# Row maxima subtracted as four extra contraction rows, a down projection with the activations stationary, and re-ordered vector, scalar and Pool work in the attention

## The chip, the cores and the metric

The kernel runs on one core of a Trainium2 chip. The metric is the device time of one execution in microseconds; three runs of the kernel before took 1431.07, 1431.39 and 1433.14 us (median 1431.39). Five engines work side by side, each with its own instruction queue, and wait for one another by semaphores: TensorE (PE, matrix products), VectorE (DVE), ScalarE (ACT), GpSimd (POOL) and SyncE (SP, here only the issuer of DMAs).

## The reference

Two layers of a bidirectional encoder trunk on x of 512 tokens by 1024 channels, everything in float32. The part that the change touches is the softmax of two attention groups and the last projection:

```python
p = h @ W_in                       # hyena channels | GQA q, k, v | MLA q-rank, kv-rank, rope key
# GQA: 8 query heads, 2 kv heads, d 64.   MLA: 4 heads, nope 64 + shared rope 32, v 64
s  = einsum(q, k) * scale          # per head, 512 queries x 512 keys
pr = softmax(s, axis=-1)           # subtracts the row maximum
o  = einsum(pr, v)
y  = concat(rms(hyena), rms(gqa), rms(mla)) @ w_out
x += rms_norm(y, mix_post_norm)
f  = (gelu(dwconv3(h @ W_g)) * dwconv3(h @ W_u)) @ w_down      # 2816 -> 1024
x += rms_norm(f, ffn_post_norm)    # the last layer's x is the output
```

## The kernel before, in words

Activations lie transposed in SBUF, channels on partitions: `xT` is [128, 8, 512], chunk c holding channels 128c to 128c+127 of all 512 tokens. A product in float32 accuracy is made of three products of a faster type (fp32r): operand and weight are each split into a rounded high part and a low remainder, and `triple` or `tiles` (L1105 to L1107, L1138 to L1140) issue high x high, high x low and low x high. Weights come in items of at most 8 tiles of 128x128: SP loads an item into `raw` (two slots), ScalarE rounds it into `wh` (`hi`, L611), Pool takes the remainder `wl` (`lo`, L527). Some items (`third`) use a third pair of buffers, `xh` and `xl`; `freed` says after which item a buffer may be overwritten. Nothing is scheduled by a planner: each engine's program is written out by hand, in Python loops, and its order is the order of the queue.

**Attention.** The 12 heads (8 GQA, then 4 MLA) run one after the other, each in two passes. In the first, `peaks(h, ...)` (L1304) makes the scores of 128 queries at a time, with queries on the partitions, in banks 0 and 1; VectorE takes each row's negated maximum into `nm[:, h % 2, qc]` (`maxima`, L1816). In the second, `scores(h, sc)` makes the same scores with 128 keys on the partitions and all 512 queries along the row, so that `exp` gives the transposed probabilities that the product with V wants. The maximum belongs to a column there, so it cannot be a bias of the exponential. It is added in the product: Pool multiplies the identity with the maxima, `shift(h)` (L564), into `diag`, [128, 512], whose column q holds only the maximum of query q, and TensorE adds `ones_r` times `diag` to each score tile (L1328). A GQA tile is therefore three products of 512 columns (`ka` x `Q2`, `kb` x `Q2`, `ones_r` x `diag`), where `Q2[h % 3]` stacks the high and the low part of q on the two halves of the partitions and `ka`, `kb` hold the key's high and low part twice. An MLA tile is one full float32 product (L1325) and the `diag` product. While head h's score tiles are made, the `peaks` of head h+1 are made between them. `values` (L1445) are the products with V of a pair of heads, `denominators` (L1456) the sums over keys, from `row_sums` of VectorE (L1826); `bank7` makes the MLA projections in nine pieces between the heads; `group(g)` (L1401), `group_square`, `group_sum`, `group_norm`, `group_hi` and `group_lo` are the RMSNorm of the three groups ahead of `w_out`.

**The last down projection.** As in the first layer, output chunk m (of 8) is accumulated over the 22 chunks of the hidden activations `fh`, `fl` with weights stationary and 512 tokens moving: 8 x 22 x 3 matmuls. Chunk 7 is done in two halves of 256 tokens (`last_item`), so that the norm of the first half can start while the second is made. Then follow the sum of squares over partitions (`stat_post`, L1090 and L1093), the root on ScalarE (`post`), gain times root and the residual (`last_stream`, with Pool's `add` taking every second chunk), the turn back to tokens on partitions with 32 transposes of 128x128 (L1576), the copies to `xout` (L1027) and eight DMAs of 256 KB.

## Time and profile before

| | |
|---|---|
| median of 3 runs | 1431.39 us |
| the profiled execution, its own time | 1426.5 us |
| span, first to last instruction | 1424.7 us |
| mean granted clock of TensorE | 0.994 of full speed |
| PE busy | 1368.3 us, 96% of the span |
| DVE, ACT, POOL busy | 915.4, 587.7, 554.1 us |

The matmuls are pipelined: the profile gives each its full latency, so that the durations of neighbours overlap, and what one costs in a row of them is the distance from its start to the next start. A full float32 product appears as two matmul records. The attention of the first layer lies at about 166 to 292 us, that of the second at 864 to 993 us; the last down projection ends at 1411 us.

### The profile page before, as it was taken

The page shows a single profiled execution, that of the slowest core. Times are in us where ns is not written, and L with a number is a line of the kernel's source. Part 1 is how long each engine was busy: PE and PEld are TensorE (multiplying, and loading weights), DVE is VectorE, ACT ScalarE, POOL GpSimd, SP SyncE. Part 2 cuts the span into 40 slices and gives each one's busy share as a digit, 9 for nine tenths or more (in the row PEclk, how much of TensorE's full clock was granted, in tenths as well). Part 3 has the DMA queues.
Part 4 walks back from the last instruction along what each step waited for, and adds up shares of the span by engine and source line. Part 5 has one row for each costly group of instructions (what it writes and reads, how often), then busy time and mean ns, then how long its engine had stood idle before and what let it go on. Part 6 is the DMA issues. An engine that isn't in the chain of part 4 may idle for free. (4 is left out here: it accounts for less than half of the span.)

```text
span 1424.7 us, 15494 instructions
## 1 busy us (share of the span) xinstructions
PE 1368.3 (96%) x5988; PEld 1027.0 (72%) x5988; DVE 915.4 (64%) x992; ACT 587.7 (41%) x864; POOL 554.1 (39%) x287
## 2 busy tenths in 40 slices
PE   7999989999999999999989998998999999999998
PEld 5587654378888888788866785444888888887886
DVE  6776976547777787611286788665478877874213
ACT  5322455545543434422352225454464344343323
POOL 3221333046444444444552224320554444444444
PEclk9999999999999999999999999999999999999999
DMA  7313201022233333233341222110223333333332
GB/s 250 97 30 81 67 10 52 1 61 73 85 94 95 97 89 103 82 93 95 101 143 49 60 49 57 30 30 15 75 75 89 89 99 94 89 99 87 92 97 84
DMA packets 205538, 112.53 MB, mean 79 GB/s; under 512 B 15303, under 2 KB 202425, under 8 KB 204570
## 3 DMA queue, kind: packets, MB, share of 16 engines
q1 hardware_dynamic: 205466, 111.54, 27.0%
q8 instruction: 48, 0.79, 0.2%
q14 instruction: 24, 0.20, 0.0%
HBM read 105.63 MB, written 2.10 MB: 76 GB/s over the span
## 5 line engine op out<-in xcount | busy, mean ns | idle before, releaser
L527 POOL TENSOR_TENSOR wl<-raw,wh 128x1024 fp32r<-128x1024 f32 x172 | 421.5, 2451 | 628.2 <-ACT wh L611 628.2
L611 ACT ACTIVATE wh<-raw 128x1024 fp32r<-128x1024 f32 x172 | 182.1, 1059 | 519.8 <-PE ps L1140 493.8
L1138 PE MATMUL ps<-gh,wh 128*128 128x512 f32 (+1 forms) x848 | 340.7, 402 | 0.0
L1140 PE MATMUL ps<-gh,wl 128*128 128x512 f32 (+1 forms) x848 | 334.7, 395 | 0.0
L1139 PE MATMUL ps<-gl,wh 128*128 128x512 f32 (+1 forms) x848 | 334.6, 395 | 0.0
L1138 PEld LDWEIGHTS ps<-gh,wh 128*128 128x128 f32 (+1 forms) x848 | 158.3, 187 | 43.3 <-issue 3.9
L1139 PEld LDWEIGHTS ps<-gl,wh 128*128 128x128 f32 (+1 forms) x848 | 158.3, 187 | 40.5 <-issue 2.4
L1140 PEld LDWEIGHTS ps<-gh,wl 128*128 128x128 f32 (+1 forms) x848 | 158.2, 187 | 39.1
L1599 DVE TENSOR_TENSOR acc<-acc,sq 128x512 f32<-128x512 f32 x24 | 60.2, 2510 | 190.1 <-ACT sq L655 190.1
L2030 DVE SCALAR_TENSOR_TENSOR cv<-pad,pm,cv 128x512 f32<-128x512 f32 x88 | 127.4, 1447 | 70.0 <-ACT cv L989 70.0
L1138 PE MATMUL ps<-fh,wh 128*128 128x512 f32 x308 | 121.7, 395 | 0.6 <-POOL wl L527 0.6
L1139 PE MATMUL ps<-fl,wh 128*128 128x512 f32 x308 | 121.5, 395 | 0.0
L1140 PE MATMUL ps<-fh,wl 128*128 128x512 f32 x308 | 121.5, 395 | 0.0
L2017 DVE TENSOR_TENSOR fl<-fprod,fh 128x512 fp32r<-128x512 f32 x44 | 98.9, 2247 | 13.2 <-ACT fh L1006 13.2
L1816 DVE TENSOR_REDUCE nm<-ps 128x1 f32<-128x512 f32 x96 | 64.0, 687 | 42.5 <-PE ps L1304 42.0
L564 POOL TENSOR_TENSOR diag<-ident,nm 128x512 fp32r<-128x512 f32 x24 | 28.9, 1204 | 128.7 <-DVE nm L1816 66.5
L2033 DVE SCALAR_TENSOR_TENSOR cv<-pad,pm,cv 128x512 f32<-128x512 f32 x88 | 70.5, 802 | 3.1
L989 ACT ACTIVATE cv<-pad,pm 128x512 f32<-128x512 f32 x88 | 70.5, 803 | 0.0
L1138 PEld LDWEIGHTS ps<-fh,wh 128*128 128x128 f32 x308 | 58.0, 188 | 15.0 <-issue 1.5
L1140 PEld LDWEIGHTS ps<-fh,wl 128*128 128x128 f32 x308 | 58.0, 188 | 13.6
L1139 PEld LDWEIGHTS ps<-fl,wh 128*128 128x128 f32 x308 | 58.0, 188 | 13.5
L2025 DVE TENSOR_TENSOR pad<-ps,rbc 128x512 f32<-128x512 f32 x88 | 56.4, 683 | 8.1 <-ACT rbc L622 8.1
(288 smaller groups left out, 2242.0 us busy)
## 6 DMA issues: line engine op xcount, KB each, us to landing
raw<-w_up SPq DMA_DIRECT2D x86, 512.0 KB, 3.8
raw<-w_down SPq DMA_DIRECT2D x32, 512.0 KB, 3.8
raw<-w_in SPq DMA_DIRECT2D x30, 512.0 KB, 4.1
raw<-w_out SPq DMA_DIRECT2D x16, 512.0 KB, 3.8
raw<-w_down SPq DMA_DIRECT2D x16, 384.0 KB, 3.4
xio<-x SPq DMA_DIRECT2D x4, 512.0 KB, 4.7
win<-c_win SPq DMA_DIRECT2D x2, 1024.0 KB, 5.5
TF<-c_tf SPq DMA_DIRECT2D x2, 1024.0 KB, 8.7
```

Source lines behind the costliest of these rows:

```text
L527: nc.gpsimd.tensor_tensor(l, raw[:, slot, :], h.bitcast(F32), ALU.subtract).then_inc(S["lo_ready"], 1)
L611: A(xh[:] if third(lay, n) else wh[:, slot, :], raw[:, slot, :], ACT.Copy).then_inc(S["hi_ready"], 1)
L989: A(cv[:, k, :], pad[:, k, 1:T + 1], ACT.Identity, scale=pm[:, bass.ds(col + j + (PM["ffn_w1"] + k * FC), 1)], bias=pm[:, bass.ds(col + j ...
L1138: mm(ps[0:cols, bank, :], w_hi, x_hi, start=start and k == 0, stop=False)
L1139: mm(ps[0:cols, bank, :], w_hi, x_lo, start=False, stop=False)
L1140: ins = mm(ps[0:cols, bank, :], w_lo, x_hi, start=False, stop=stop and k == tile_n - 1)
L1599: tt(acc[:], acc[:], sq[:, m % 2, :], ALU.add).then_inc(S["ysq_used"], 1)
L1816: nc.vector.reduce_max(nm[:, h % 2, qc:qc + 1], ps[:, N_BANK(h, qc), :], AX.X, negate=True).then_inc(S["nmax"], 1)
L2017: tt(fl[:, j:j + 1, :], fprod[:].rearrange("p (o t) -> p o t", o=1), fh[:, j:j + 1, :].bitcast(F32), ALU.subtract).then_inc(S["f_lo"], 1)
L2025: tt(pad[:, k, 1:T + 1], ps[:, UP_BANK(j, k), :], rbc[:], ALU.mult).then_inc(S["f_evac"], 1)
L2030: V.do(stt(out=c, in0=pad[:, k, 0:T], scalar=pm[:, bass.ds(col + j + (PM["ffn_w0"] + k * FC), 1)], in1=c, op0=ALU.mult, op1=ALU.add))
L2033: stt(out=c, in0=pad[:, k, 2:T + 2], scalar=pm[:, bass.ds(col + j + (PM["ffn_w2"] + k * FC), 1)], in1=c, op0=ALU.mult, op1=ALU.add).then_i ...
```

## The change

**Maxima as rows.** After the fourth `maxima` of a head, TensorE turns `nm[:, h % 2, :]`, [128, 4], with the identity into [4, 128] (`turn_maxima`), right behind `scores(h - 1, 3)`. VectorE multiplies this by a block identity into four rows of 512 (`max_row`): row c holds the maxima of queries 128c to 128c+127 in its own 128 columns and zeros elsewhere. These rows lie under the queries (partitions 64 to 67 of the new buffer `q3` for GQA, 96 to 99 of `mqf` for MLA), and four rows of ones lie under the keys, in `kb` and `mkf`. The `diag` product and Pool's `shift` are gone. For GQA the second product is now the key's low part (64 rows) with the whole q, copied by Pool into `q3` (`q_again`), plus the four rows. `klo` writes `kb` twice instead of four times, and the ones.

```diff
+                def turn_maxima(h):
+                    pe.wait_ge(S["nmax"], lay * N_TILES + (h + 1) * TC)
+                    mm(ps[ROW(h), N_BANK(h, TC - 1), 0:P], nm[:, h % 2, :], ident[:], start=True, stop=True).then_inc(S["nm_tr"], 1)
+
                     if h < GH:
                         mm(ps[:, bank, :], ka[:, h // 4, keys], Q2[h % 3], start=True, stop=False)
-                        mm(ps[:, bank, :], kb[:, h // 4, keys], Q2[h % 3], start=False, stop=False)
+                    if sc == 0:
+                        ...
+                        pe.wait_ge(S["nm_row"], lay * HEADS + h + 1)
+                    if h < GH:
+                        ins = mm(ps[:, bank, :], kb[row, h // 4, keys], q3[row, h % 2, :], start=False, stop=True)
                     else:
-                        mm(ps[:, bank, :], mkf[0:MD, h - GH, keys], mqf[0:MD, h - GH, :], start=True, stop=False)
-                    if sc == 0:
-                        pe.wait_ge(S["shift"], lay * HEADS + h + 1)
-                    mm(ps[:, bank, :], ones_r[:], diag[:, h % 2, :], start=False, stop=True).then_inc(S["s_tile"], 1)
+                        ins = mm(ps[:, bank, :], mkf[row, h - GH, keys], mqf[row, h - GH, :], start=True, stop=True)
+                    ins.then_inc(S["s_tile"], 1)
...
+                def max_row(h):
+                    rows = ROW(h)
+                    dst = q3[rows, h % 2, :] if h < GH else mqf[rows, h - GH, :]
+                    ...
+                    dve.wait_ge(S["nm_tr"], lay * HEADS + h + 1)
+                    tt(dst.rearrange("p (c n) -> p c n", c=TC),
+                       ps[rows, N_BANK(h, TC - 1), 0:P].unsqueeze(1).to_broadcast([TC, TC, P]),
+                       ident[rows, rows].unsqueeze(2).to_broadcast([TC, TC, P]), ALU.mult).then_inc(S["nm_row"], 1)
```

**Orders.** On VectorE each `max_row(h + 1)` stands behind `maxima(h + 1)`, at heads 4, 6, 8 and 10 behind `pair_out` too, at head 7 behind a copy of `bank7`; `row_sums(1)` moves behind `maxima(4)`, `row_sums(9)` and `row_sums(10)` into head 11; the group sums move ahead of the `row_sums` of their head; `group_norm(1)` is split in two. Two of the four low parts of the MLA weights (`uql`, `ukl`) move from VectorE to Pool. On Pool the two first `w_out` items move from the beginning and the middle of the attention behind head 9. On ScalarE the group squares move ahead of `inverse` and `group_hi(1)` is split. On TensorE one quarter of the last `values` comes ahead of `denominators(4)`.

On TensorE, head 3 of the first layer and what stands just ahead of it, before (q2 is a slot of `Q2`):

```order
L1328 MATMUL ps<-diag,ones_r 128x512
L1445 MATMUL ps<-probT0,vg 64x512
L1445 MATMUL ps<-probT1,vg 64x512
L1445 MATMUL ps<-probT0,vg 64x512
L1445 MATMUL ps<-probT1,vg 64x512
L1322 MATMUL ps<-q2,ka 128x512 [waits p_ready]
L1323 MATMUL ps<-q2,kb 128x512
L1328 MATMUL ps<-diag,ones_r 128x512 [waits shift]
L1304 MATMUL ps<-ka,q2 128x512 [waits q2lo,q2hi,nmax]
L1304 MATMUL ps<-ka,q2 128x512 [waits nmax]
```

and now:

```order
L1393 MATMUL ps<-ident,nm 4x128 [waits nmax]
L1543 MATMUL ps<-probT0,vg 64x512
L1543 MATMUL ps<-probT1,vg 64x512
L1543 MATMUL ps<-probT0,vg 64x512
L1543 MATMUL ps<-probT1,vg 64x512
L1412 MATMUL ps<-q2,ka 128x512 [waits p_ready]
L1420 MATMUL ps<-q3,kb 128x512 [waits nm_row,q3]
L1388 MATMUL ps<-ka,q2 128x512 [waits q2lo,q2hi,nmax]
L1388 MATMUL ps<-ka,q2 128x512 [waits nmax]
```

The product with `diag` is gone from each tile, the turn of the maxima stands once per head ahead of the products with V, and the tile's second product carries the wait for the rows.

On VectorE, from the end of `maxima(4)` (head 3) to the reductions of the next head, before:

```order
L1816 TENSOR_REDUCE nm<-ps 128x1 [waits n_tile] x3
L1826 TENSOR_TENSOR tsum<-uc 128x1024 [waits den_mm,p_ready]
L1930 TENSOR_TENSOR yt<-kr,rope 32x512 [waits kr_in]
L1931 TENSOR_TENSOR yt<-krs,rope 32x512
L1933 TENSOR_TENSOR kr<-yt 32x512 [waits dve_self]
L1816 TENSOR_REDUCE nm<-ps 128x1 [waits n_tile,shift,dve_self]
```

and now:

```order
L1910 TENSOR_REDUCE nm<-ps 128x1 [waits n_tile] x3
L1920 TENSOR_TENSOR tsum<-probT1 128x1024 [waits p_ready]
L1894 TENSOR_TENSOR q3<-ps,ident 4x512 [waits nm_tr]
L1902 TENSOR_TENSOR ckl<-ckv,ckh 128x512 [waits mhi]
L2025 TENSOR_TENSOR yt<-kr,rope 32x512 [waits kr_in]
L2026 TENSOR_TENSOR yt<-krs,rope 32x512
L2028 TENSOR_TENSOR kr<-yt 32x512 [waits dve_self]
L1920 TENSOR_TENSOR tsum<-uc 128x1024 [waits den_mm,p_ready,dve_self]
L1910 TENSOR_REDUCE nm<-ps 128x1 [waits n_tile,nm_tr]
```

`row_sums(1)` (tsum from probT1), which `denominators(0)` waits for, now stands between the maxima of head 4 and their row, and `ckl` has come here too.

**The last down projection.** In the last layer an item is now the 128 rows of one hidden chunk kk with all 1024 output channels, 22 items in place of 24. `last_down` holds the activations still (128 hidden by 128 tokens) and moves 512 output channels: all 8 banks accumulate at once, bank 2tt + dh for token block tt and half dh, and the last two chunks (`TAIL`) are done bank by bank. The output has tokens on the partitions; `xT` is turned beforehand, in 8 groups of four transposes between the up projection's items (`turn_stream`), and ScalarE copies each to `xres`. Item LAST (kk 21) uses `xh`, `xl`.

```diff
+            def last_down(lay):
+                def part(kk, tt, dh):
+                    h, l = weights(lay, I_DOWN + kk)
+                    bank, rows, cols = 2 * tt + dh, slice(tt * P, (tt + 1) * P), slice(dh * T, (dh + 1) * T)
+                    mm(ps[:, bank, :], fh[:, kk, rows], h[:, cols], start=kk == 0, stop=False)
+                    mm(ps[:, bank, :], fl[:, kk, rows], h[:, cols], start=False, stop=False)
+                    return mm(ps[:, bank, :], fh[:, kk, rows], l[:, cols], start=False, stop=kk == FC - 1)
+                ...
+                for kk in range(FC - TAIL):
+                    ready(kk)
+                    for tt in (0, 2, 3, 1):
+                        ...
+                        for dh in range(2):
+                            ins = part(kk, tt, dh)
+                    ins.then_inc(S["pe_item"], 1)
+                for kk in range(FC - TAIL, FC):
+                    ready(kk)
+                for tt in range(TC):
+                    for dh in range(2):
+                        for kk in range(FC - TAIL, FC):
+                            ins = part(kk, tt, dh)
+                        ins.then_inc(S["y_done"], 1)
...
+            for tt in range(TC):                                   # ScalarE
+                s0, s1, part, log, r = (st[:, tt, i:i + 1] for i in range(5))
+                act.wait_ge(S["y_done"], 2 * tt + 1)
+                C.do(A(yt[:, 0, :], ps[:, 2 * tt, :], ACT.Square, accum_out=s0))
+                ...
+                C.do(A(yt[:, 1, :], ps[:, 2 * tt + 1, :], ACT.Square, accum_out=s1))
+                ...
+                C.do(A(log, s1, ACT.Ln, bias=part, scale=1.0 / DM))
+                C.join()
+                A(r, log, ACT.Exp, scale=-0.5).then_inc(S["r_inv"], 1)
...
+            for i in range(TC):                                    # VectorE
+                for dh in range(2):
+                    dve.wait_ge(S["y_sq"], 2 * i + dh + 1)
+                    ...
+                    tt(ytmp[dh], ps[:, 2 * i + dh, :], cv[:, dh, :], ALU.mult).then_inc(S["y_gain"], 1)
+                dve.wait_ge(S["r_inv"], i + 1)
+                for dh in range(2):
+                    dve.wait_ge(S["y_gain"], 2 * i + dh + 1)
+                    x = xres[2 * i + dh]
+                    stt(out=x, in0=ytmp[dh], scalar=st[:, i, 4:5], in1=x, op0=ALU.mult, op1=ALU.add).then_inc(S["o_done"], 1)
```

The sum over channels is now along the row, so ScalarE takes it while squaring; `stat_post`, `last_stream`, Pool's adds, the transposes of the tail and the copies to `xout` are gone. At the program's end TensorE has, before (the last triple of chunk 7, its statistics, the first of the 32 transposes):

```order
L1090 MATMUL ps<-acc,ones_r 128x256 [waits rms_post]
L1093 MATMUL ps<-sq,ones_r 128x256 [waits ysq]
L1576 MATMUL ps<-ident,xT 128x128 [waits x_own]
L1576 MATMUL ps<-ident,xT 128x128
L1576 MATMUL ps<-ident,xT 128x128 [waits x_new]
```

and now (the bank-by-bank end: wh is item kk 20, xh item kk 21):

```order
L1239 MATMUL ps<-wh,fh 128x512 [waits hi_ready,lo_ready,f_lo,f_hi]
L1240 MATMUL ps<-wh,fl 128x512
L1241 MATMUL ps<-wl,fh 128x512
L1239 MATMUL ps<-xh,fh 128x512
L1240 MATMUL ps<-xh,fl 128x512
L1241 MATMUL ps<-xl,fh 128x512
```

Nothing of TensorE's follows these six once they have been made for the eighth bank.

## Rows read from the trace of the kernel before

**Rows 1.** Waits of PE, whole run: total us, times, longest (the attention's lines).

```profile
PE ps L1401 <- DVE acc L1909: 5.7, 6, 1.2
PE ps L1304 <- DVE nm L1816: 5.4, 6, 1.5
PE ps L1328 <- POOL diag L564: 4.4, 4, 1.9
PE ps L1304 <- POOL q L555: 2.9, 3, 1.3
PE ps L1138 <- DVE yl L1924: 2.8, 2, 1.4
PE ps L1456 <- ACT cv L622: 1.7, 2, 0.8
PE ps L1322 <- DVE kb L1801: 1.5, 2, 1.0
```

**Rows 2.** Both attentions by window: length, busy (count) by engine, PEclk, DMA.

```profile
166.00:292.00 126.00, 113.50 (x425) 57.84 (x425) 82.79 (x109) 66.53 (x113) 31.95 (x23) 0.99 0.08 24
864.00:993.00 129.00, 115.87 (x428) 59.17 (x427) 83.11 (x109) 67.26 (x113) 32.41 (x23) 0.97 0.09 24
...
184.00:186.00 2.00, 2.00 (x7) 1.57 (x6) 1.51 (x3) 1.12 (x2) 0.00 (x0) 0.54 0.00 0
```

**Rows 3.** Timeline, PE, head 2 to 3: start us, us, instruction.

```profile
198.38 0.39 PE L1304 MATMUL ps<-ka,q 128*128 128x512 f32 x1
...
199.08 0.40 PE L1328 MATMUL ps<-diag,ones_r 128*128 128x512 f32 x1
```

**Rows 4.** Timeline, DVE: the maximum of the product that starts at 198.38.

```profile
198.81 0.69 DVE L1816 TENSOR_REDUCE nm<-ps 128x1 f32<-128x512 f32 x1 [0.24 <-PE ps L1304]
```

**Rows 5.** Timeline, PE: two MLA score tiles of the last head, start to start.

```profile
272.40 1.02 PE L1325 MATMUL ps<-mqf,mkf 96*128 96x512 f32 x2
...
273.49 1.02 PE L1325 MATMUL ps<-mqf,mkf 96*128 96x512 f32 x2
```

**Rows 6.** Timeline, PE: four 128x128 transposes and the next product.

```profile
164.07 0.60 PE L1375 MATMUL ps<-ident,cv 128*128 128x128 f32 x4
164.50 0.59 PE L1279 MATMUL ps<-sq,ones_r 128*128 128x512 f32 x1
```

**Rows 7.** Timeline, PE: denominators of a pair, and the next score product.

```profile
222.81 1.94 PE L1456 MATMUL ps<-tsum,ones_r 128*64 128x512 f32 x8
224.68 0.50 PE L1322 MATMUL ps<-q,ka 128*128 128x512 f32 x1
```

**Rows 8.** DVE: 32 partitions from PSUM (timeline); row sums (group: busy, mean ns).

```profile
176.28 0.68 DVE L1691 SCALAR_TENSOR_TENSOR kr<-ps,rbc 32x512 f32<-32x512 f32 x1
...
L1826 DVE TENSOR_TENSOR tsum<-probT 128x1024 f32<-128x1024 f32 x9 | 12.9, 1435 | 4.3 <-PE ps L1456 4.3
```

**Rows 9.** Timeline, PE and ACT, the end of the program.

```profile
1408.10 0.59 PE L1090 MATMUL ps<-acc,ones_r 128*128 128x256 f32 x2
...
1408.78 0.47 PE L1105 MATMUL ps<-fh,xh 128*128 128x256 f32 x1
...
1411.12 0.59 PE L1090 MATMUL ps<-acc,ones_r 128*128 128x256 f32 x2
...
1421.81 0.38 ACT L1027 ACTIVATE xout<-ps 128x256 f32<-128x256 f32 x1 [0.29 <-PE ps L1576]
```

**Rows 10.** Timeline, ACT and DVE: 512-column operations as in the new tail.

```profile
159.93 0.63 ACT L763 ACTIVATE sq<-cq 128x512 f32<-128x512 f32 x1 [3.86 <-DVE cq L1694]
...
175.50 0.75 DVE L1775 SCALAR_TENSOR_TENSOR cq<-cq,pm,rr 128x512 f32<-128x512 f32 x1
```

**Rows 11.** The last down projection's items: rounding, remainder, landing of a load.

```profile
1312.43 1.06 ACT L611 ACTIVATE wh<-raw 128x1024 fp32r<-128x1024 f32 x1 [4.51 <-PE ps L1140]
...
1313.57 2.40 POOL L527 TENSOR_TENSOR wl<-raw,wh 128x1024 fp32r<-128x1024 f32 x1 [3.16 <-ACT wh L611]
...
raw<-w_down SPq DMA_DIRECT2D x32, 512.0 KB, 3.8
```

More of the change, by code:

```diff
@@ L264, in build @@
         ysave = probT0
+        xres = [rope[:, i, :] for i in range(5)] + [w3[:, 0:T], w3[:, T:2 * T], h2[:, 0:T]]
+        ytmp = [sq[:, 0, :], sq[:, 1, :]]
         groot = [rbc[:], cv[:, 1, :], rbc[:]]
@@ L492, in _ @@
                     item(lay, I_UP + 2 * j + 1, w_up[bass.ds(lay, 1), :, :, bass.ds(DFF + j * P, P)])
+                if lay == DEPTH - 1:
+                    for kk in range(FC):
+                        item(lay, I_DOWN + kk, a["w_down"][lay:lay + 1, kk * P:(kk + 1) * P, :].rearrange("o p (c n) -> o p c n", n=P))
+                    sp.wait_ge(S["f_prod"], DEPTH * FC)
+                    sp.dma_start(cv[:].rearrange("p t n -> p (t n)"), a["ffn_post_norm"][lay, :].partition_broadcast(P)
+                                 ).then_inc(S["g_in"], 16)
+                    continue
                 for m in range(0, DC - 1, 2):
@@ L529, in add @@
             def add(lay, b):
-                last = (lay, b) == (DEPTH - 1, 1)
                 for half in range(2):
                     for c in range(DC):
-                        if (c % 2 == 0 if last else c == half == 0):
+                        if c == half == 0:
                             continue
@@ L594, in _ @@
                 add(lay, 0)
-                for n in range(I_UP + 2, ITEMS + 1 if lay < DEPTH - 1 else ITEMS - 1, 2):
+                for n in range(I_UP + 2, ITEMS + 1 if lay < DEPTH - 1 else LAST, 2):
                     for slot in range(2):
@@ L861, in group_root, with group_hi @@
                     act.wait_ge(S["gstd"], lay * 3 + g + 1)
-                def group_hi(g):
+                def group_hi(g, cs=None):
                     src, _, n, c0 = GROUPS[g]
-                    for c in range(n):
+                    for c in cs or range(n):
                         act.wait_ge(S["y_norm"], lay * DC + c0 + c + 1)
@@ L1009, in _ @@
                 tables("natural_log_exp_and_others")
+                if lay == DEPTH - 1:
+                    for n in range(I_DOWN + 3, LAST + 1):
+                        hi(lay, n, n % 2)
+                    continue
                 for m in range(DC):
@@ L1909, in group_sum, with group_norm @@
                         tt(acc[:], acc[:], sq[:, k % 2, :], ALU.add).then_inc(S["gsq_used"], 1)
-                def group_norm(g):
+                def group_norm(g, cs=None):
                     src, _, n, c0 = GROUPS[g]
                     dve.wait_ge(S["gstd"], lay * 3 + g + 1)
-                    for c in range(n):
+                    for c in cs or range(n):
                         stt(out=src[:, c, :], in0=src[:, c, :], scalar=par("g_out", c0 + c), in1=groot[g], op0=ALU.mult,
@@ L1963, in _ @@
                         maxima(h + 1)
+                    if h == 3:
+                        row_sums(1)
+                    if h == 2 or h % 2 and h + 1 < HEADS and h != 7:
+                        max_row(h + 1)
                     if h in B7_FIRST and B7[B7_FIRST[h]][0] in ("pe", "v"):
@@ L1967, in _ @@
                         pair_out((h - 4) // 2)
-                    if h:
+                        if h + 1 < HEADS:
+                            max_row(h + 1)
+                    if h == 7:
+                        max_row(h + 1)
+                    if h == 3:
+                        mla_lo(1)
+                        rotate_kr()
+                    if h == 5:
+                        group_sum(0)
+                        group_sum(1)
+                    if h == 9:
+                        group_sum(2)
+                        group_sum(3)
+                    if h == 10:
+                        group_sum(5)
+                    if h == 11:
+                        group_norm(1, [0, 1])
+                    if h not in (0, 2, 11):
                         row_sums(h - 1)
```

230 lines of the change are left out of this document (126 added, 104 removed).

## The prediction, made before the changed kernel was run

> **What bounds the kernel now.** I read the busy shares first: TensorE (PE) is busy 96% of the span at a mean clock of 0.994, the others at most 64%. PE's program is therefore the path, and a term counts only as PE time taken away or added, PE waiting, PE's clock, or the start and the tail of the program. Next I read PE's waits [rows 1]: the seven rows that belong to the attention sum to 24.4 us over both layers (5.7 + 5.4 + 4.4 + 2.9 + 2.8 + 1.7 + 1.5), none above 1.9. Then the windows over both attentions [rows 2]: PE clock 0.99 and 0.97, VectorE (DVE) busy 83 of 126 us, Pool 32. And then the timeline of the end [rows 9]: the last product of the down projection is over at 1411.12, the last copy starts at 1421.81, the span ends at 1424.7. All sums are made against the profiled execution's own 1426.5 us; the median of the runs lies 4.9 us above it, and I carry that over.
>
> **The change part by part.**
>
> *The product with `diag`.* From 198.38 to 199.08 three matmuls start, 0.233 us each [rows 3]. Twelve heads, four tiles, two layers make 96 of the removed ones: 96 x 0.233 = 22.4 us less. Four more contraction rows in the remaining product, and 68 in place of 128 rows in the second GQA product, cost nothing: time goes by the moving columns, since the 96-row MLA product with its `diag` product takes 1.09 us a tile [rows 5], that is 0.86 for 512 columns of full float32.
>
> *The turn of the maxima.* 24 full float32 products of 128 columns. None is in the trace; a quarter of 0.86 is 0.215, and with its whole latency exposed it would be about 0.5. I take 0.22, the nearer row: +5.2 us (bounds 5 to 12). It cannot be below nothing, as it is an added instruction.
>
> *The new waits.* The turn waits for the fourth maximum. A product that starts at 198.38 has its maximum at 198.81 + 0.69 = 199.50 [rows 4], while PE, after that product and the two of a GQA tile, is ready 3 x 0.233 later, at 199.08: 0.42 us, about 0.47 with the semaphore, at the eight heads where the tile before the turn is GQA. At MLA heads PE has 0.23 + 0.86 = 1.09 us of its own and waits for nothing. That makes 3.8 us a layer. What queues behind the turn on PE is the products with V or the denominators; who waits for it is only `max_row`. `max_row` itself reads PSUM and writes 4 partitions of 512; the nearest row, 32 partitions of 512 from PSUM, takes 0.68 [rows 8], and bounds of 0.4 and 1.0 change little: the denominators of a pair take 1.87 us on PE [rows 7], and the turn and the row (0.22 + 0.68 and two semaphores, about 1.1) go by beside them. Only at head 1, where nothing but one product lies between, is some 0.5 us open, and it takes the place of the 1.9 us wait for Pool [rows 1].
>
> *The other stops, per layer.* What I count as left: 0.4 at the first `peaks`; 1.4 at head 0, because the norm of `cq` and the copy of `kr` still stand ahead of `maxima(1)`; 0.5 for the row of head 1; 1.0 for `cql`, now behind that row; 1.3 at head 3, where the rotary work of `bank7` stands ahead of `maxima(4)`; 1.0 at `denominators(0)`, since `row_sums(1)`, 1.4 us by the mean [rows 8], now comes behind `maxima(4)`, less the turn; 1.0 at `group(2)`; 0.5 for the rest. With the 3.8 above it is 10.9 a layer, 21.7 in all against 24.4: -2.7 us. Gone are the group sums of groups 0 and 1, the wait for Pool's low part of q, the wait for `yl` and that for the root ahead of the denominators. The bounds are wide: -17 if only the turn's wait stays, +10 if the queue of VectorE falls behind.
>
> *VectorE and Pool.* VectorE takes on 12 x 0.68 = 8.2 us a layer and loses two low parts and two of four `kb` operations; at most 91 us [rows 2] in an attention of some 114. Pool loses 12 products and gains 8 copies of half the partitions; at 32 us of 126 [rows 2] nothing waits for it but the first heads. Both are free as long as their slack lies where it is needed.
>
> *The clock.* The granted clock fell to 1.2 GHz after the 1.9 us wait in the first layer (0.54 granted in 184 to 186 [rows 2]), and both windows together lost (1 - 0.99) x 126 + (1 - 0.97) x 129 = 5.1 us. With waits of at most 1.4 us I give back two thirds: -3.4 us (bounds 0 and -5.1, and a loss of as much again if the new row of short waits brings it down more often).
>
> *The turn of x.* 32 transposes between the up projection's items. Four of them start at 164.07 and the next product at 164.50 [rows 6]: 0.108 each, +3.4 us. The copies stand on ScalarE, less than half busy there. The Trainium skill ("TensorE: Matmul & The Clock Gate", Part 4: PE-mode transpose) gives about 275 ns for one in a kernel's context; by its figure the term would be 8.8 us. The row here shows the start-to-start distance, which is what counts in a queue, and I go by it.
>
> *The down projection.* The same number of full products, 22 x 8 x 3. The two halves of chunk 7 go: 132 products of 256 columns at 0.120 against 66 at 0.233, and the statistics between them, 1408.10 to 1408.78 [rows 9]: -1.1 us together. An item is 24 products, 5.6 us, and needs 1.06 + 2.40 us of ScalarE and Pool [rows 11], so PE does not wait in the row. The end does: chunks 20 and 21 must both be ready when 19 is done. The slot of 21 is free when the remainder of 19 is, 3.6 us after PE left 17; the load lands 3.8 us later [rows 11], and Pool can start on 21 only behind 20, at about 9.3, ending at 11.8 when PE is there at 11.2: +0.6 us. At the start of the projection, banks of the last up items are touched last (token block 1 at 4.2 us into the first item): nothing.
>
> *The tail.* Before, 1424.7 - 1411.12 = 13.6 us. Now, after the last product: 0.2 until ScalarE starts, a square 0.63 [rows 10], the logarithm and the exponential of one column (not in the trace; between 0.17 and 0.42 each, I take 0.25) with their joins 0.7, two operations of 0.75 on VectorE [rows 10], and from the last release to the end as before, 1424.7 - 1421.81 - 0.38 = 2.5 us [rows 9]. This is 5.5; VectorE's own row, with a product from PSUM behind the last square, adds 0.3: 5.8 us, -7.8. Bounds 4.8 and 8.5, the second if VectorE (2 x 0.68 + 2 x 0.75 = 2.9 us for a token block) is late against PE's 12 x 0.233 = 2.8.
>
> **Sum.** -22.4 + 5.2 - 2.7 - 3.4 + 3.4 - 1.1 + 0.6 - 7.8 = -28.2: own time 1398.3 us, median 1403.2.
>
> **The rivals.**
>
> *A, VectorE sets the pace.* Its chain through a head (four maxima, row, row sums, and what stands between) is then the longest, and the `diag` time comes back as PE waiting. For it: the largest attention waits are for VectorE [rows 1], and it takes on 8 us. Against: 83 of 126 us busy [rows 2]. The three attention terms would cancel, leaving -3.4 - 4.9: 1423.
>
> *B, all stops go but the turn's.* The order was moved at each row of [rows 1], and PE's own time around the pair products (1.87 us against four times 0.43 [rows 5, 7]) makes PE later, and so VectorE earlier, than I count. Another 14.2 us: 1389.
>
> *C, slower: the round trip is on the path at every head.* PE, VectorE, PE, VectorE, PE follow one another once per head. If VectorE has other work ahead of `max_row`, as `pair_out` is at four heads and `row_sums` at one, the row comes after the pair products: 0.7 for what stands ahead, and 0.9 for turn and row uncovered, 24 x 1.6 = 38 us. 1403 + 38 = 1441. From 28.2 / 24 = 1.2 us a head the change is lost. Against it: 1.87 us of cover [rows 7], and the largest thing ahead of a row is row sums at one head.
>
> *D, transposes are not pipelined between other products.* By the length of the first row of [rows 6], 0.60 for four of which three distances are 0.32, each would cost 0.28, +5.4 us: 1409. The Trainium skill's 275 ns ("TensorE: Matmul & The Clock Gate", Part 4: PE-mode transpose) would come to the same.
>
> *E, the change does not do what it says*: if the last down projection with its eight open banks stalls at each chunk by the 1.06 + 2.40 us of its preparation, because buffers come free later than I read, the 7.8 us are used up from 0.4 us a chunk. 1411.
>
> **How the numbers follow.** The forecast 0.58 (its own range 1394 to 1411), A 0.13, B 0.13, C 0.06, D 0.06, E 0.04. Less than 0.2% (2.9 us, about what this measurement tells from nothing) is left only between A and C. Faster 0.92, same 0.03, slower 0.05. For 8 times in 10 the range reaches to B, and towards A without holding it: 1390 to 1420.
>
> **What would show it.** Right: no product of `ones_r` with a [128, 512] tile; about 0.45 us of PE waiting for VectorE's maxima ahead of each of eight turns a layer; no wait for the rows above 0.6 us but at the first heads; attentions 11 to 12 us shorter each; transposes 0.11 us apart; about 0.6 us of waiting once, ahead of the last two chunks; 5.8 us from the last product to the end. Wrong: PE waits for `max_row` at most heads (C), VectorE busy over 85% of the attention and PE waiting for maxima within a head (A), PE waits for Pool inside the last projection (E), or a mean clock below 0.97 in either attention.

## The result and the profile after

| | before | after |
|---|---|---|
| median of the runs, us | 1431.23 (1431.06 to 1433.14, 4 runs) | 1396.65 (1393.99 to 1399.51, 4 runs) |
| ratio, 95% interval | | 0.9756 [0.9732, 0.978] |
| profiled execution, its own time, us | 1426.5 | 1398.35 |
| its span, us; mean granted clock | 1424.7; 0.994 | 1396.6; 0.993 |

Faster by 34.6 us; the forecast was 1403.2 by the median and 1398.3 by the profiled execution's own time. The second came out to 0.1 us, which is luck: as shown below, the waits fell by 5.4 us more than forecast, while the turn of the maxima, the clock between the layers and the layout of the operands together came out some 8 us dearer.

TensorE's waits in the changed kernel (whole run; us in total, times, longest), to be laid beside [rows 1]:

```profile
PE ps L1144 <- DVE gl L1681: 7.3, 14, 1.6
...
PE ps L1388 <- DVE nm L1910: 5.2, 6, 1.5
PE ps L1393 <- DVE nm L1910: 5.1, 16, 0.3
...
PE ps L1554 <- DVE tsum L1920: 2.6, 2, 1.3
...
PE ps L1388 <- POOL q L576: 1.4, 2, 0.8
...
PE ps L1496 <- DVE acc L2004: 1.1, 2, 0.6
PE ps L1420 <- DVE q L1894: 0.9, 2, 0.4
PE ps L1239 <- POOL xl L549: 0.8, 1, 0.8
```

The attention's rows (L1388, L1393, L1554, L1496, L1420) now sum to 16.3 us against 24.4. New is L1393, the turn: sixteen waits, eight a layer as forecast, of 0.3. The waits for `diag`, `kb`, `yl` and for the roots are gone, and four of the six for group sums. `cql`, for which the forecast had 1.0 a layer, does not appear.

The windows over both attentions, then the place between the layers (window, its length, busy time and count per engine, PE's clock, DMA), beside [rows 2]:

```profile
166.00:278.00 112.00, 103.74 (x399) 48.98 (x400) 85.38 (x118) 66.08 (x112) 25.28 (x22) 1.00 0.10 28
855.00:968.00 113.00, 104.82 (x398) 48.93 (x398) 85.38 (x118) 66.09 (x112) 24.65 (x22) 0.98 0.10 28
700.00:726.00 26.00, 22.90 (x110) 17.95 (x111) 23.55 (x39) 13.78 (x26) 16.25 (x15) 0.80 0.53 182
```

The first attention runs at 1.00. But between the layers, where the kernel before had 1.00 in the same window, the clock is 0.80: half of the time spent at 1.2 GHz is 5.1 us there, in a stage that the change does not touch.

```profile
700.00:726.00 26.00, 22.62 (x161) 20.03 (x160) 16.64 (x32) 12.71 (x24) 17.63 (x17) 1.00 0.53 184
```

TensorE's timeline at the turn of head 1 (start, length, line, tiles, idle time before and its releaser), beside [rows 3]:

```profile
179.15 0.40 PE L1420 MATMUL ps<-q,kb 68*128 68x512 f32 x1
179.86 0.38 PE L1393 MATMUL ps<-ident,nm 128*4 128x128 f32 x2 [0.31 <-DVE nm L1910]
180.18 0.50 PE L1412 MATMUL ps<-q,ka 128*128 128x512 f32 x1
181.12 0.47 PE L1420 MATMUL ps<-q,kb 68*128 68x512 f32 x1 [0.44 <-DVE q L1894]
```

From 179.15 to 179.86 are 0.71, less the product's 0.23 are 0.48: the forecast's 0.47 (the view shows 0.31 of it as idle, since it lets the product end later). The turn itself takes 0.32 before the next product starts (179.86 to 180.18), where the forecast had 0.22. No third product of [rows 3] follows a score's second, and the one of 68 rows still costs one 0.23 (the median over the 32 that a product of `peaks` follows). The turn of x, beside [rows 6], and the wait ahead of chunks 20 and 21 (the four transposes last 0.60 together and stand 0.109 apart, so that one alone lasts 0.60 - 3 x 0.109 = 0.27):

```profile
1072.77 0.60 PE L1231 MATMUL ps<-ident,xT 128*128 128x128 f32 x4
1073.12 0.48 PE L1177 MATMUL ps<-gh,wh 128*128 128x512 f32 x1
```

```profile
1379.91 0.47 PE L1239 MATMUL ps<-wh,fh 128*128 128x512 f32 x1 [0.77 <-POOL xl L549]
```

And the end of the program, beside [rows 9]:

```profile
1390.86 0.40 PE L1241 MATMUL ps<-xl,fh 128*128 128x512 f32 x1
...
1391.29 0.60 ACT L1070 ACTIVATE yt<-ps 128x512 f32<-128x512 f32 x1 [0.29 <-PE ps L1241]
...
1391.79 0.19 ACT L1070 ACTIVATION_READ_ACCUMULATOR yt<-ps 128x1 f32 x1
1392.06 0.69 DVE L2163 TENSOR_TENSOR sq<-ps,cv 128x512 f32<-128x512 f32 x1 [0.15 <-ACTq L1072]
1392.10 0.30 ACT L1073 ACTIVATE st<-st 128x1 f32<-128x1 f32 x1
1392.42 0.20 ACT L1075 ACTIVATE st<-st 128x1 f32<-128x1 f32 x1
1392.66 0.75 DVE L2168 SCALAR_TENSOR_TENSOR w<-sq,st,w 128x512 f32<-128x512 f32 x1
1393.33 0.74 DVE L2168 SCALAR_TENSOR_TENSOR h<-sq,st,h 128x512 f32<-128x512 f32 x1
```

The last product is over at 1391.09 (its start and 0.23), the span at 1396.55: 5.5 us against 13.6.

### The profile page after: what moved, and what is told of

Same layout as the page of the kernel before. It is cut to its first block, busy times and chain, and to the rows that moved or that the text cites. A ratio compares the mean times of both kernels' runs of the same rounds, so it can differ in the third digit from the quotient of the medians.

```text
span 1396.6 us, 15257 instructions
## 1 busy us (share of the span) xinstructions
PE 1352.3 (97%) x5866; PEld 1006.3 (72%) x5866; DVE 899.8 (64%) x995; ACT 583.7 (42%) x865; POOL 531.9 (38%) x275
## 4 chain that ended last, share of the span: by engine, by line
PE 77%; DVE 14%; ACT 2%; issue 2%; POOL 2%; DMA 1%; SPq 1%; POOLq 0%; DVEq 0%; ACTq 0%
PE ps L1177 16%; PE ps L1178 16%; PE ps L1179 16%; PE ps L1239 3%; PE ps L1240 3%; PE ps L1241 3%; DVE nm L1910 2%; PE ps L1543 2%; PE ps L1338 2%; PE ps L1312 2%; PE ps L1422 2%; PE ps L1554 1%; DVE p L1817 1%; PE ps L1388 1%; DVE gl L1681 1%
## 5 line engine op out<-in xcount | busy, mean ns | idle before, releaser
L549 POOL TENSOR_TENSOR wl<-raw,wh 128x1024 fp32r<-128x1024 f32 x170 | 417.3, 2455 | 684.4 <-ACT wh L640 672.8
L1690 DVE TENSOR_TENSOR acc<-acc,sq 128x512 f32<-128x512 f32 x18 | 45.2, 2511 | 112.7 <-ACT sq L684 112.7
L2120 DVE TENSOR_TENSOR fl<-fprod,fh 128x512 fp32r<-128x512 f32 x44 | 95.0, 2159 | 17.7 <-ACT fh L1042 17.7
L2163 DVE TENSOR_TENSOR sq<-ps,cv 128x512 f32<-128x512 f32 x8 | 5.5, 688 | 104.0 <-ACTq L1067 102.9
L1239 PE MATMUL ps<-wh,fh 128*128 128x512 f32 x168 | 66.5, 396 | 1.0 <-POOL xl L549 0.8
L1241 PE MATMUL ps<-wl,fh 128*128 128x512 f32 x168 | 66.3, 395 | 0.0
L1240 PE MATMUL ps<-wh,fl 128*128 128x512 f32 x168 | 66.3, 395 | 0.0
L1177 PE MATMUL ps<-fh,wh 128*128 128x512 f32 x154 | 61.0, 396 | 0.3 <-POOL wl L549 0.3
L1179 PE MATMUL ps<-fh,wl 128*128 128x512 f32 x154 | 60.9, 396 | 0.0
L1178 PE MATMUL ps<-fl,wh 128*128 128x512 f32 x154 | 60.9, 396 | 0.0
```

Of the source, the lines that this page charges most:

```text
L549: nc.gpsimd.tensor_tensor(l, raw[:, slot, :], h.bitcast(F32), ALU.subtract).then_inc(S["lo_ready"], 1)
L1177: mm(ps[0:cols, bank, :], w_hi, x_hi, start=start and k == 0, stop=False)
L1178: mm(ps[0:cols, bank, :], w_hi, x_lo, start=False, stop=False)
L1179: ins = mm(ps[0:cols, bank, :], w_lo, x_hi, start=False, stop=stop and k == tile_n - 1)
L1239: mm(ps[:, bank, :], fh[:, kk, rows], h[:, cols], start=kk == 0, stop=False)
L1240: mm(ps[:, bank, :], fl[:, kk, rows], h[:, cols], start=False, stop=False)
```

## The experiments

All times are medians. Each kernel ran beside the kernel before on the same chip, which gave 1428.22 us (17 runs, from 1423.3 to 1432.93) beside `again`, `attn_only`, `down_only` and `no_diag`, 1426.31 (15) beside `st8`, `turn_cover`, `old_orders` and `dve_load`, 1427.76 (11) beside `before_pad`, `st12` and `st24`, and 1427.49 (9) beside `head0`. A stage table, worked out from starts of instructions and the clock records of each profiled execution, serves all of them. Each entry is the stage's length, and behind it the time lost in it at 1.2 GHz (half of the time spent there), both in us. An attention is counted from its first `peaks` to `group(2)`, the output and up projection from there to the first down product.

| kernel | attention 0 | attention 1 | output and up 0 | output and up 1 | down 0 | last product to end |
|---|---|---|---|---|---|---|
| before | 124.5, 1.7 | 127.1, 3.4 | 293.9 | 294.7 | 124.4 | 13.7 |
| after | 110.7, 0 | 112.3, 1.7 | 294.9 | 298.3 | 124.8 | 5.7 |
| again | 112.7, 3.4 | 111.8, 1.7 | 294.9 | 298.3 | 124.8 | 5.7 |
| attn_only | 111.3, 1.7 | 110.3, 0 | 293.9 | 293.9 | 124.4 | 14.0 |
| down_only | 127.2, 3.4 | 125.3, 1.7 | 294.9 | 298.3 | 124.8 | 5.7 |
| no_diag | 120.2, 1.7 | 119.9, 3.4 | 293.9 | 293.9 | 124.5 | 15.0 |
| old_orders | 126.5, 5.1 | 127.4, 6.8 | 295.0 | 298.3 | 124.8 | 5.7 |
| dve_load | 116.1, 3.4 | 117.2, 5.1 | 294.9 | 298.3 | 124.8 | 5.7 |
| before_pad | 127.7, 3.4 | 125.2, 1.7 | 288.0 | 288.0 | 122.3 | 14.0 |
| st12 | 111.3, 1.7 | 110.7, 0 | 290.3 | 293.9 | 124.4 | 5.7 |
| st8 | 112.3, 3.4 | 111.3, 1.7 | 288.0 | 291.8 | 122.4 | 5.7 |
| st24 | 111.3, 1.7 | 112.3, 3.4 | 288.0 | 291.9 | 122.3 | 5.7 |
| head0 | 110.8, 0 | 111.9, 1.7 | 288.0 | 291.8 | 122.4 | 5.7 |
| turn_cover | 111.3, 0 | 114.2, 3.4 | 294.9 | 298.3 | 124.8 | 5.7 |

The second figure is the most that the clock can have cost, not what it did cost. Up to the first `peaks`, `again` lost 3.4 us and took 167.0, `turn_cover` lost none and took 167.1. The first attention of the same orders took 110.7 with nothing lost (after), 111.3 with 1.7 (attn_only, st24) and 112.3 and 112.7 with 3.4 (st8, again). Where TensorE waits anyway, its slower products seem to fill the waits. Figures "without the clock" below are therefore somewhat low for the kernels that lost more.

**again**: no edit.

> The changed kernel once more, unchanged, to see what moves its time between runs. Theory (clock stretches): the runs of it spread over 1394 to 1400 us, and a run's time follows its mean granted clock, 0.01 of clock being 14 us of PE at a lower rate (a run at 0.999 about 1394, one at 0.990 about 1399.5); the number of stretches at 1.2 GHz between the start and the tail is not the same in each run. The kernel before should show a higher time (1431) than its profiled 1426.5 for the same reason, at a clock near 0.990 in its plain runs. Rival (what surrounds the span): all runs have the same clock within 0.002, and the spread comes from outside the span.

1396.84 (1394.92 to 1399.38). Each run's time lies 1.7 to 1.8 above its span, so what surrounds the span is constant and the rival falls. The clock goes with most of the spread, not with all: of the 17 runs of before the quickest, 1423.3, had 0.995, and those at 0.988 took 1431.5 and 1432.0; between, runs at 0.993 lie from 1427.1 to 1429.3. A straight line through the 17 gives 8.9 us for 0.01 of clock, where the expectation had 14. With the whole loss taken out (span times clock) the 17 average 1414.8 and the four of `again` 1386.5. The profiled execution of before, 1426.5, lies within these runs.

**attn_only** and **down_only**: the diff's two halves, each on the kernel before.

> Only the attention's part of the change (maxima as rows, the new orders); the last down projection and the end stay as before. Theory: the sum of the attention terms, -22.4 + 5.2 - 2.7 - 3.4 = -23.3 us, up to -28.5 by the stage windows of the changed kernel, so 1403 to 1408 against 1431. Rival 1 (the parts help each other: the attention's gain needs the other end of the program): -15 or less. Rival 2 (the attention's gain is the clock's alone and is given back between the layers): -18.

> Only the last down projection with eight open banks, the turn of x between the up items and the new end; the attention stays as before. Theory: +3.4 for the 32 transposes, -1.1 and +0.6 in the projection, -7.8 in the tail = -4.9 us: 1426. By the windows of the changed kernel -4.7 with 5.5 us from the last product to the end. Rival (the row on record calls it E, chunks stall): no gain, 1431, with PE waiting for ScalarE or Pool ahead of chunks. Rival (transposes cost 0.28 each): +5.4 more.

1398.45 (ratio 0.9795 [0.977, 0.982]) and 1422.91 (0.9964 [0.995, 0.9978]): -29.8 and -5.3 us. The attention brings more than the forecast's 23.3, the end what was forecast. The two sum to 35.1, together they bring 31.4; the spread of the runs (four of attn_only, with clocks of 0.989 to 0.996, and twelve of down_only) covers the difference, and the stages of the table show nothing that only the two together bring.

**no_diag**:

```
-  mm(..., kb[:, h // 4, keys], Q2[h % 3], start=False, stop=False)
+  mm(..., kb[:, h // 4, keys], Q2[h % 3], start=False, stop=True).then_inc(S["s_tile"], 1)
...
-  mm(ps[:, bank, :], ones_r[:], diag[:, h % 2, :], start=False, stop=True).then_inc(S["s_tile"], 1)
```

> The kernel before without the 96 products of diag, so the maxima are found but not subtracted; Pool still makes diag, and PE asks for it only at the last tile of a head. It prices the removed product by itself. Theory (PE's time is the bill): 96 x 0.233 = 22.4 us and most of the 4.4 us of waits for Pool's shift go, some 5 us of longer waits for maxima come: -20 to -25, 1406 to 1411. Rival (VectorE's maxima are nearly the pace): PE waits for nmax within heads take half of it back, 1418 to 1422.

The kernel leaves out the subtraction of the maxima, and serves to price it. 1416.47: -11.8 us, half of the 22.4 that the products took, and a little better than the rival. TensorE's waits in this kernel:

```profile
PE ps L1304 <- POOL q L555: 8.1, 10, 2.1
PE ps L1304 <- DVE nm L1815: 8.1, 8, 1.8
...
PE ps L1400 <- DVE acc L1908: 6.2, 6, 1.1
...
PE ps L1416 <- DVE cql L1807: 3.3, 2, 1.6
```

Against [rows 1] Pool's low part of q went from 2.9 to 8.1, the maxima from 5.4 to 8.1, and `cql` is new. All waits in the attentions sum to 36.5 us, against 25.2 in the kernel before (the seven of [rows 1] and one of 0.8): 11.3 of the 22.4 us come back as waiting, and 11.1 are left, which is what the runs show.

**old_orders**: the new rows and the new end, with VectorE's and ScalarE's orders of before; what was moved on Pool and TensorE stays moved.

```
                     if h and h + 1 < HEADS:
                         maxima(h + 1)
+                        max_row(h + 1)
...                      (group sums, norms, row_sums and rotate_kr where they were before)
```

> The changed kernel with the orders of VectorE and ScalarE in the attention as they were before, and each row of maxima right behind the four maxima. It parts the new rows from the new orders. Taking the product away alone (no_diag) gave 12 us and not 22, since waits for VectorE and Pool grew. Theory (the orders are worth what no_diag missed): about 1405, the group sums' waits (5.7 us) back, and waits for the rows or the denominators at even heads. Rival 1 (the rows alone bring it, the orders little): 1398. Rival 2 (C of the forecast: with the row at the wrong place the round trip is on the path): over 1415.

1427.36, ratio 1.0001 [0.9981, 1.0021] to the kernel before: 30.5 us more than `again`, and nothing left of the change. Since the new end is in it and brings 5.3 by itself, its attention is even slower than that of before (126.5 + 127.4 against 124.5 + 127.1 in the table). With the clock's loss taken out, the table gives 121.4 and 120.6 for its attentions, against 109.9 and 110.3 in the mean of after, again and attn_only: 21.8 us are waits, and the waits of the attention's lines, 37.8 us in all against 14.6 in `again`, bear that out. The clock goes with the rest: its mean over the runs is 0.9876 against 0.9938, at most 17.7 us lost against 8.7. TensorE's waits in the first attention:

```profile
PE ps L1385 <- DVE nm L1907: 7.7, 5, 3.7
PE ps L1493 <- DVE acc L2001: 4.1, 3, 1.8
PE ps L1390 <- DVE nm L1907: 2.2, 7, 0.3
...
PE ps L1417 <- DVE q L1891: 0.4, 1, 0.4
```

The time is in the range given to rival 2 (over 1415; C itself said 1441), its mechanism is not the one at work: TensorE waits 0.4 us for a row (L1417), but 3.7 at once for a maximum of head 4, behind the rotary work, `row_sums` and `ckl` in VectorE's queue, and 1.8 for a group sum.

**dve_load**: 

```
+  V.do(tt(tsum[:, h % 2, 0, :], pT[:, 0, :], pT[:, 2, :], ALU.add))
+  V.join()
   tt(tsum[:, h % 2, :, :], pT[:, 0:2, :], pT[:, 2:4, :], ALU.add).then_inc(S["summed"], 1)
```

> The changed kernel with half of each row sum computed twice, 24 more operations of about 0.7 us on VectorE, 16.8 us in all; VectorE was busy 85 of 112 us in an attention. Theory (VectorE has slack in the middle of a head, and what waits is the latency of single steps): +2 to +5 us, at denominators and at heads with bank 7 work: 1399 to 1402. Rival (A of the forecast: VectorE sets the pace): nearly all of it shows, +14 to +17: 1411 to 1414.

1407.99: +11.2 us, between the two. Of it 2.8 and 1.8 are in the attentions without the clock (112.7 and 112.1 against the same 109.9 and 110.3), as waits for the row sums:

```profile
PE ps L1554 <- DVE tsum L1922: 7.0, 4, 2.0
```

(2.1 in `again`.) The clock may have taken 3.6 more (0.9912 in the mean against 0.9938); some 3 us stay open, within the spread of four runs (1402.46 to 1408.97). VectorE has slack, but not 8 us a layer of it at this place: the added operation stands straight ahead of the row sums, and other places were not tried.

**turn_cover**: 

```
-  if after:
+  if after and h not in (5, 7, 9):
       turn_maxima(h + 1)
...
   for part in range(2):
+      if part and 1 <= p < PAIRS - 2:
+          turn_maxima(2 * p + 4)
```

> The changed kernel with three of the eleven turns behind the first two products of the denominators (heads 5, 7, 9), so that TensorE has 0.9 us of its own work while the fourth maximum comes. Theory (the forecast's wait of 0.42 us at a turn is the latency of the maximum, and the cover behind the turn is long enough): the wait of 0.31 to 0.33 us at these six turns goes and no wait for a row comes: -2.0 us, 1395. Rival (the row is then late: turn and row take some 1.2 us by now, and 0.9 + 0.23 us of products lie between): a wait for q or mqf at the next scores, 0 us or up to +1.

1396.14, no difference from 1396.84. Its waits:

```profile
PE ps L1388 <- DVE nm L1912: 6.2, 8, 1.5
...
PE ps L1393 <- DVE nm L1912: 3.8, 12, 0.3
...
PE ps L1556 <- DVE mv L2046: 1.3, 2, 0.6
```

The turn's fell from 4.8 to 3.8, those for maxima rose from 5.2 to 6.2 and one of 1.3 is new: the row is later, and VectorE's queue hands that on. Without the clock its attentions take 222.1 us, against 220.2 in the mean of after, again and attn_only. Its four runs had a higher clock, 0.998 in the mean, so the equal medians may hide a loss of some 2 us; whether the clock was chance or the edit's doing is not shown.

**st8**, **before_pad**, **st12**, **st24**: the layout alone.

```
-  st = sb("st", [P, TC, 5])
+  st = sb("st", [P, TC, 8])          (st8; 12 and 24 in st12 and st24)
```
```
   nm = sb("nm", [P, 2, TC])
+  unused = sb("unused", [P, 32])     (before_pad)
```

> The changed kernel with the statistics tile `st` of 8 columns in place of 5 (128 bytes a partition, not 80), nothing else. In the runs so far each kernel with the new end (the changed one, its repeat, the one with the end alone) starts its projection products 0.2328 us apart, those without it 0.2319: output and up projection of layer 0 take 294.9 against 293.9 us, the down projection 124.8 against 124.4. `st` lies ahead of the operands that move through TensorE (gh, gl, fh, fl, yh, yl). Theory (where the operands lie): with 128 bytes the distance is 0.2319 again, 293.9 and 124.4 in layer 0, 297.3 in layer 1, in all 2.5 to 3 us less: 1394 by the median. Rival (it is the new code on another engine, or the eight banks): 294.9 stays, 1397.

1379.71, ratio 0.9667 [0.9645, 0.9689]: -17.1 us against `again` (16 by the two ratios) and not -3. The theory named the right tile and the wrong size, so three more kernels were made to find the rule.

> The kernel before with an unused tile of 128 bytes a partition ahead of gh, nothing else. With `st` at 128 bytes (st8) the changed kernel's projection products start 0.2267 us apart and not 0.2328, and it runs 17 us shorter; it is to be seen whether that has to do with the change. Counting tiles in the order in which they are declared, rounded up to 32 bytes, wh lies at a multiple of 256 bytes, and gh at 128 beyond one before, 224 beyond one in the changed kernel, 0 beyond one in st8; products of gh with xh, whose remainders are equal in all, start 0.227 apart in all of them. Theory (equal remainders of 256 bytes for the two operands): before falls by 3312 products x 0.0052 = 17 us less some in waits, to 1411, and all products with wh and wl to 0.227. Rival (it is the tile st or the new end): 1428 stays.

> The changed kernel with `st` of 192 bytes a partition, so that gh lies 64 beyond a multiple of 256 and wh at one. Theory (equal remainders): products with wh start 0.232 to 0.233 apart as at 128 and 224, time 1394 to 1397. Rival (the remainder counts by itself, not against the other operand; 64 may be as good as 0): 0.227 or less, 1380.

> The changed kernel with `st` of 384 bytes a partition: gh now lies at a multiple of 1024 bytes, as wh does, while in st8 it lay 256 beyond a multiple of 512. Theory (256 bytes is the size that counts): as st8, 0.2267 between products and 1380. Rival (more of the address counts): shorter distances still, down to 0.2133 for 512 columns at 2.4 GHz, which would be 3400 x 0.013 = 45 us less; or longer ones.

1410.68 (0.9878 [0.9858, 0.9897]), 1388.38 (0.9714) and 1377.13 (0.9645 [0.9624, 0.9666]). An unused tile makes the kernel before 17 us faster, so this has nothing to do with the change. A window of 100 us in the up projection of layer 0, with the count of products, of before, after, st12, before_pad and st24 in turn:

```profile
400.00:500.00 100.00, 100.00 (x432) 1.00 0.33 95
```
```profile
400.00:500.00 100.00, 100.00 (x431) 1.00 0.32 92
```
```profile
400.00:500.00 100.00, 100.00 (x438) 1.00 0.32 95
```
```profile
400.00:500.00 100.00, 100.00 (x442) 1.00 0.33 95
```
```profile
400.00:500.00 100.00, 100.00 (x443) 1.00 0.33 97
```

443 products where 432 were, with the clock at 1.00 and TensorE busy throughout in all. Two rows of the timeline of st24, a triple of products apart, take 0.68 us for three, where the changed kernel's take 0.70:

```profile
500.29 0.39 PE L1177 MATMUL ps<-gh,wh 128*128 128x512 f32 x1
...
500.97 0.39 PE L1177 MATMUL ps<-gh,wh 128*128 128x512 f32 x1
```
```profile
500.21 0.40 PE L1177 MATMUL ps<-gh,wh 128*128 128x512 f32 x1
...
500.91 0.40 PE L1177 MATMUL ps<-gh,wh 128*128 128x512 f32 x1
```

Where both operands have the same remainder of 256 bytes (by the declared sizes, rounded up to 32 bytes) the distance is 0.227; at 128 apart 0.232, at 224 apart 0.2335 in the mean. st12, 64 apart, refutes the plain rule: `gl` with `wh` goes at 0.227 there, `gh` with `wl` at 0.230, `gh` with `wh` at 0.2325, and it gains half. A control stands in every kernel: the products with `xh`, whose remainder is that of `gh` whatever `st` is, have a median distance of 0.227 in before and in the changed kernel too, beside 0.232 and more for those with `wh`. st24 is st8 within the spread, and at no layout did a mean distance fall below 0.226, so its rival falls. Why the remainders matter stays open.

**head0**: on st24, VectorE's order at head 0.

```
+  copy(kb[GD:GD + TC, :, :] ...)     (the row of ones, ahead of maxima(0))
   maxima(0); klo(); max_row(0)
-  norm(5, [cq 0, cq 1]); evac(kr); maxima(1)
+  norm of cq 0; maxima(1, [0, 1]); norm of cq 1; maxima(1, [2, 3])
   max_row(1); mla_lo(0)
+  evac(kr)
```

> st24 with VectorE's order at head 0 changed: the row of ones is copied ahead of the maxima of head 0, the first two maxima of head 1 stand between the two halves of the norm of cq, and the copy of kr behind the low part of cq. In every run so far TensorE waits 1.5 us there (peaks of head 1), by VectorE's queue: norm 1.54 and kr 0.68 stand ahead of the maximum that is asked for. Theory: the wait falls from 1.5 to 0.2 us in both layers and the row of head 0 comes 0.5 us earlier; no new wait for cql: -3 to -3.5 us against st24, 1374. Rival (the next step in VectorE's queue takes the wait over: the row of head 1 or cql is late by what the first gained): 1377. Rival (the clock falls after the wait of 1.5 us, so it gives back 1.7 us a layer more): 1371.

1378.44 (0.9669 [0.9642, 0.9696]) against 1377.13: nothing. TensorE's waits name where it went:

```profile
PE ps L1412 <- ACT probT L931: 3.4, 2, 1.7
PE ps L1388 <- DVE nm L1908: 2.5, 5, 0.9
```

The 1.5 us for the maximum are gone in both layers, and 1.7 us for ScalarE's exponentials stand one product later. ScalarE, not VectorE, was the second to be late there.

## Why the prediction was right, and which terms were off

| term | forecast, us | measured, us | from |
|---|---|---|---|
| products with `diag` | -22.4 | -22.4 | 96 fewer, distances as before |
| turn of the maxima | +5.2 | +7.5 | 24 x 0.31, from a turn's start to the next product's |
| waits in the attention | -2.7 | -8.1 | 16.3 against 24.4, as the view counts them |
| clock in the attention | -3.4 | -3.4 | stage table, 5.1 to 1.7, at most |
| rest of the attention | 0 | -2.2 | what is left of the attentions' -28.6; not parted by any run |
| clock elsewhere | 0 | +3.2 | last down product of layer 0 to the second attention: 158.8, and 155.6 in again, with nothing lost |
| turn of x | +3.4 | +3.4 | 298.3 - 294.9, and 0.108 apart |
| layout of the operands | not seen | +2.4 | layer 0: 294.9 - 293.9, 124.8 - 124.4; 1.0 again in layer 1's up projection |
| last down projection | -0.5 | -0.2 | 124.5 to 124.3, wait 0.77 for 0.6 |
| tail | -7.8 | -8.1 | 13.6 to 5.5 |
| all else | 0 | -0.3 | start, stage between the layers, layer 1's projection |
| from profile to median | +4.9 | -1.7 | 1396.65 - 1398.35 |

Without its last row the measured column sums to -28.2. The attentions became 13.8 and 14.8 us shorter, where the forecast's own sign of being right was 11 to 12: it gained more there than it knew, and lost in stages that it had put at nothing.

**The waits** are the term that was mis-sized most. Nearly half of that is a way of counting. The eight turns a layer were right in number and size, 0.48 us each by distance for 0.47, but the view shows 0.32 of it as idle, so that they enter the 16.3 with 5.1 us where the forecast booked 7.5. The guesses around them came to 11.2 us for 14.2. Head 0 was right (1.5 for 1.4, and the reason given for it, the norm and `kr`, is shown by head0). Too high were `cql`, 0 for 1.0, head 3, 0.9 for 1.3, and `group(2)`, 0.55 for 1.0; too low were `denominators(0)`, 1.3 for 1.0, and the first `peaks`, 0.7 for 0.4, which still wait for the low part of q that the forecast called gone. The late work of [rows 1] was taken out of VectorE's queue more fully than the guesses allowed. The prediction named this as rival B; 3 of its 14.2 us were gone.

**The turn** cost 0.31 to 0.33 us from its start to the next product at 22 of its 24 places (at the other two the next product waits for the row sums), where 0.22 was taken, within the stated bounds of 5 to 12 us. The clock's loss and the waits being rough, the rest of -2.2 says no more than that these terms do not add up to the last us.

**The orders were priced far too low.** The forecast gave the removed product 22.4 us and all orders together 2.7. The runs show another split: product removed with the old orders, -11.8 (no_diag); rows in place of `diag` and the new end with the old orders, nothing, so that the rows alone cost more than they bring, 2.3 us by the stage table and some 6 by the medians less the end's -5.3 (old_orders); rows with the new orders, -29.8 (attn_only). What rival A described, the product's time coming back as waiting, is thus true of the old orders and false of the new ones; its reason, that VectorE is full, is not what the trace of old_orders shows, where single late steps of up to 3.7 us make the waits. The total came out because the whole diff was forecast, not its parts. Which of the moved operations brings how much is not parted.

**The clock.** In the attention its loss fell as forecast, from 5.1 to 1.7 us, but in that execution it fell elsewhere too, between the layers, which the forecast had not. `again`, the same kernel, lost nothing there and 3.4 in its first attention, where the first execution lost none: the place changes from execution to execution. By the means over the runs the loss is 11.8 us before (0.9918), 7.3 and 8.7 in the two sets of the changed kernel (0.9948 and 0.9938). So the -3.4 of one trace against another was in part a draw, and its agreement with the forecast is luck.

**The carry.** 4.9 us were added since before's profiled execution lay that far under its median, as if that were a constant between the two. A good part is clock: that execution lost at most 0.006 x 1425 = 8.5 us, where the 17 later runs of before lost 11.8 in the mean; the changed kernel's profiled execution lost 9.8, the runs of `again` 8.7. Put at the means, a difference of -28.2 becomes -28.2 - 3.3 - 1.1 = -32.6, and measured are -34.6 in the first set and -31.4 in the second. The clocks of the first set's runs of before are not known, and that set's median, 1431.2, lies 3 us above the later one's, 1428.2: that part stays open.

**Transposes** stood 0.108 apart (rival D, 0.28 each, would show as some 9 us in place of 3.4). The Trainium skill ("TensorE: Matmul & The Clock Gate", Part 4: PE-mode transpose) gives about 275 ns for a 128x128 bf16 transpose in one kernel's context. This trace agrees if that is the duration of one, 0.27 here in float32; from start to start they take 0.109, and it is the start-to-start distance that a term of the sum needs: 3.4 us for 32 are 0.11 each.

**The end.** Rival E is out: one wait of 0.77, where 0.6 was forecast. Of the tail's parts the square was 0.60 and 0.19 for reading its sum, the logarithm 0.30, the exponential 0.20 (0.25 each assumed), and VectorE was in step.

## What to carry to other kernels

- Removing work from the busiest engine is worth its time only if the others' queues are in step with it. Price a reordering by running the removal with the old order: here 12 us against 30, and with the rows in place of the product nothing.
- When a stop is cleared, the next one may stand close behind: neither of the two reorderings tried after the change (turn_cover, head0) moved the median. Look for the second latest releaser before you move anything.
- Compare the distance of identical products between two kernels before explaining a few us. A tile of 80 bytes ahead of the operands cost 2.4 us here (1.0 + 0.4 in layer 0, 1.0 in layer 1), and tiles of 128 and 384 bytes in its place, or an unused one of 128 in the kernel before, give 17 to 20: st24, at 1377.13 us, beats both kernels.

## What was not expected of the hardware

- The distance of 512-column products of `float32r` operands depends on where the two operands lie to one another: 0.227 us where their addresses have the same remainder of 256 bytes, 0.232 and 0.2335 at 128 and 224 apart, some of each at 64 apart. The remainders are worked out from the declared sizes; no other differences were tried, and the reason is open. 256-column products show no such step (means of 0.117 to 0.121 in all layouts where no wait stands between).
- More short waits went with a lower clock in `old_orders`: 21.8 us more waiting, and a mean clock of 0.9876 against 0.9938, at most another 9 us. It is no rule yet: `turn_cover` waits some 2 us more than `again` and had 0.998.
- Time at 1.2 GHz is not lost in full where TensorE waits anyway: 3.4 us of it ahead of the first `peaks` changed nothing (167.0 against 167.1), and over 17 runs 0.01 of clock went with 8.9 us and not 14.
